# Dividing one more product of a fast matrix multiplication in a hybrid decoder trunk: product 5 in groups 2 to 18

## What is computed

```python
def reference(x, norm_g, w_in, conv_w, conv_b, w_a_out, w_b_out, w_o, final_g):
    h = rmsnorm(x, norm_g[0])                        # x: 1024 positions x 1024 channels
    proj = h @ w_in[0]                               # 1024 x 12288
    b_a, c_a, x_a, z_a, q, k, v, z_b, g_a, g_b = jnp.split(proj, split_points, axis=-1)
    y_a = short_conv_branch(b_a, c_a, x_a, z_a, conv_w[0], conv_b[0], w_a_out[0])
    y_b = retention_branch(q, k, v, z_b, w_b_out[0]) # rotary(q), rotary(k), decay, chunks of 128
    merged = jax.nn.sigmoid(g_a) * y_a + jax.nn.sigmoid(g_b) * y_b
    return rmsnorm(x + merged @ w_o[0], final_g)
```

## Time and profile before

| | |
|---|---|
| median of 3 runs | 1365.6 us |
| the profiled execution's own time | 1365.87 us |
| its span, first to last instruction | 1364.1 us |
| TensorE busy (share of the span) | 1351.8 us (99%) |
| VectorE busy | 1060.0 us (78%) |
| ScalarE, GpSimd busy | 608.3 us, 413.7 us |
| mean DMA rate | 172 GB/s |

### The profile page before, as it was taken

The page is one execution under the profiler, slowest core; times in us unless marked ns, Lnnn a source line. Parts: engine busy times, 40 slices in busy tenths (PEclk is TensorE's granted clock), DMA queues, the critical chain, the costliest instruction groups (busy, mean ns, idle before and its releaser), DMA issues.

```text
span 1364.1 us, 17294 instructions
## 1 busy us (share of the span) xinstructions
PE 1351.8 (99%) x6642; PEld 1142.7 (84%) x6642; DVE 1060.0 (78%) x1097; ACT 608.3 (45%) x821; POOL 413.7 (30%) x381
## 2 busy tenths in 40 slices
PE   9999999999999999999999999999999999999997
PEld 7788888888888888888888888888888888888886
DVE  6898465677878777678888778748776998788887
ACT  6843233433333333333333433438778433433445
POOL 0100112344444554444443444315444001100002
PEclk9999999999999999999999999999999999999999
DMA  9646445344433433476666666757768699945443
GB/s 333 216 132 214 141 110 166 95 108 109 109 101 86 108 93 99 136 183 172 176 162 166 147 166 179 223 201 252 267 223 267 141 332 308 235 158 201 162 85 124
DMA packets 112979, 234.81 MB, mean 172 GB/s; under 512 B 7680, under 2 KB 50816, under 8 KB 108032
## 3 DMA queue, kind: packets, MB, share of 16 engines
q1 hardware_dynamic: 104112, 194.87, 42.2%
q0 software_dynamic: 8640, 38.80, 16.0%
q10 hardware_dynamic: 144, 0.02, 0.0%
HBM read 169.70 MB, written 55.57 MB: 165 GB/s over the span
## 4 chain that ended last, share of the span: by engine, by line
PE 92%; ACT 2%; issue 1%; DVE 1%; DMA 1%; POOL 1%; SPq 1%; POOLq 0%; ACTq 0%; DVEq 0%
PE psum L2625 15%; PE psum L2627 15%; PE psum L2628 15%; PE psum L2768 7%; PE psum L2766 7%; PE psum L2767 7%; PE psum L2549 3%; PE psum L2551 3%; PE psum L2550 3%; PE psum L2538 3%; PE psum L2540 3%; PE psum L2541 3%; PE psum L2670 2%; PE psum L2672 2%; PE psum L2671 2%
## 5 line engine op out<-in xcount | busy, mean ns | idle before, releaser
L1146 ACT ACTIVATE slots<-work 128x1024 fp32r<-128x1024 f32 (+1 forms) x166 | 169.5, 1027 | 418.0 <-PE psum L2628 292.1
L2625 PE MATMUL psum<-hc,slots 128*128 128x512 f32 x912 | 355.0, 389 | 0.0
L2627 PE MATMUL psum<-hc,slots 128*128 128x512 f32 x912 | 354.9, 389 | 0.0
L2628 PE MATMUL psum<-hc,slots 128*128 128x512 f32 x912 | 354.8, 389 | 0.0
L2628 PEld LDWEIGHTS psum<-hc,slots 128*128 128x128 f32 x912 | 171.2, 188 | 35.8
L2625 PEld LDWEIGHTS psum<-hc,slots 128*128 128x128 f32 x912 | 171.2, 188 | 35.3 <-issue 0.4
L2627 PEld LDWEIGHTS psum<-hc,slots 128*128 128x128 f32 x912 | 171.2, 188 | 34.8
L1435 ACT ACTIVATE last_slot<-arena 128x1024 fp32r<-128x1024 f32 x112 | 118.6, 1062 | 163.0 <-PE psum L2768 157.3
L2766 PE MATMUL psum<-last_slot 128*128 128x512 f32 (+1 forms) x452 | 175.3, 388 | 0.0
L2768 PE MATMUL psum<-last_slot 128*128 128x512 f32 (+1 forms) x452 | 175.0, 387 | 0.0
L2767 PE MATMUL psum<-last_slot 128*128 128x512 f32 (+1 forms) x452 | 175.0, 387 | 0.0
(11 more groups left out here) (228 smaller groups left out, 2496.1 us busy)
## 6 DMA issues: line engine op xcount, KB each, us to landing
work<-w_channel SPq DMA_DIRECT2D x80, 512.0 KB, 4.0
work<-w_channel POOLq DMA_DIRECT2D x40, 512.0 KB, 5.5
arena<-w_last SPq DMA_DIRECT2D x19, 1024.0 KB, 7.9
qk<-qk_scratch SPq DMA_DIRECT2D x32, 512.0 KB, 3.4
arena<-w_last POOLq DMA_DIRECT2D x9, 1024.0 KB, 10.5
v_raw<-value_scratch SPq DMA_DIRECT2D x32, 256.0 KB, 3.9
arena<-gate_scratch SPq DMA_DIRECT2D x16, 512.0 KB, 6.8
value_c<-w_value SPq DMA_DIRECT2D x10, 512.0 KB, 4.8
```

Of the source, the lines that this page charges most:

```text
L1146: nc.scalar.activation(slots[:, u % SLOTS, 0, 0:columns_of(u)], src, ACT.Copy, scale=-1.0 if negated(u) else 1.0).then_inc(w_hi, 1)
L2625: nc.tensor.matmul(bank, slot[:, 0, w], x_high, start=product in STARTS and j == 0, stop=False, skip_group_check=True)
L2627: nc.tensor.matmul(bank, slot[:, 0, w], x_low, start=False, stop=False, skip_group_check=True)
L2628: last = nc.tensor.matmul(bank, slot[:, 1, w], x_high, start=False, stop=j == 3, skip_group_check=True)
```

## The change

Product 5 is divided like product 4, in groups 2 to 18 (`FIFTHS`), as two units 5a (place 3) and 5b (`FIFTH_HALF`). x's combinations for the quarters of product 5 are made in group 0 and kept in HBM (`hx_d`, `kept_d`). The buffer `hx` holds those of product 5 and of product 4 in turn: two loads (512 KB for T4, 1024 KB for T1 and T2) twice in each group. T3 stays in the place of a quarter of x, as before. S1 of groups 1 to 19 is no longer added by GpSimd but made in buffer e by a load of quadrant 3 and an adding transfer of quadrant 2. Rotation steps are at other places. The PSUM bank for 5's inner sums is the other group's set.

```diff
-UNIT_TABLE = [(g, p) for g in range(GROUPS) for p in (0, 1, 2, 3, 4, 5, 6, LAST_HALF, THIRD_HALF)
+FIFTHS = range(2, GROUPS - 1)
+UNIT_TABLE = [(g, p) for g in range(GROUPS) for p in (0, 1, 2, 3, FIFTH_HALF, 4, 5, 6, LAST_HALF, THIRD_HALF)
...
-    ROLES.append(dict(a=r["c"], b=r["b"], c=r["a"], d=r["e"], e=r["d"]))
+    ROLES.append(dict(a=r["c"], b=r["b"], c=r["a"], d=r["d"], e=r["e"]))
...
+        def load_hx(product):
+            n = int(product == 5)
+            sp.dma_start(hx[:, 2].bitcast(F32), hx_d[n, :, 2]).then_inc(t4_in, 16)
+            sp.dma_start(hx[:, 0:2].bitcast(F32), hx_d[n, :, 0:2]).then_inc(t1_t2_in, 16)
...
+            if g in FIFTHS:
+                sp.wait_ge(unit_done, ended_at(g - 1) + 1)
+                load_hx(5)
...
-                sp.wait_ge(w_ready, unit_at(g, 5) + 1)
-                load_work(g + 1, "d", 3)
+                sp.wait_ge(w_ready, fifth_ended_at(g) + 1)
+                load_work(g + 1, "e", 3)
...
+                if g in FIFTHS:
+                    sp.wait_ge(unit_done, fifth_ended_at(g) + 1)
+                    load_hx(4)
...
         def s1(g):
+            if g:
+                work_loaded(g, "e")
+                pool.dma_start(work[ROLES[g]["e"]][:, :], w_channel[g, 2], accum_op=ALU.add).then_inc(s1_in, 16)
...
         def s2(g):
+            if g:
+                pool.wait_ge(s1_in, 16 * g)
...
+            if g in FIFTHS:
+                second_sums(g, 5)
             if g in THIRDS:
                 second_sums(g, 3)
...
+                elif n == 3 and halved_product(g, 5):
+                    second_first(g, 5)
+                elif n == FIFTH_HALF:
+                    second_rest(g, 5, range(1))
+                    low(u + 2)
+                    second_rest(g, 5, range(1, 3))
+                    add(g, 5)
...
-                    for step in {0: (0,), 2: (1, 2, 3, 4, 5)}.get(p, ()):
+                    for step in ({0: (0,), 1: (1, 2, 3, 4), 2: (5,)} if g in FIFTHS else {0: (0,), 2: (1, 2, 3, 4, 5)}).get(p, ()):
                         turn(last, 0, step)
                     if p == 3:
                         turned(last, 0)
-                    for step in {3: (0, 1, 2, 3), 4: (4, 5)}.get(p, ()):
+                    for step in ({2: (0, 1), 4: (2, 3, 4, 5)} if g in FIFTHS else {3: (0, 1, 2, 3), 4: (4, 5)}).get(p, ()):
                         turn(last, 1, step)
-                    if p == 4:
+                    if p == (5 if g in FIFTHS else 4):
                         turned(last, 1)
...
+            if product != 3 and g in FIFTHS:
+                pe.wait_ge(t4_in, 16 + 16 * hx_loads(g, product))
             product_of_quarters(u, 2, second(product, "T4"), direct_quarter(g, product, 2)).then_inc(unit_done, 1)
```

More of the change, by code:

```diff
@@ L191 @@
     r = ROLES[-1]
[L192 removed]
+    ROLES.append(dict(a=r["c"], b=r["b"], c=r["a"], d=r["d"], e=r["e"]))
 LOADED = [{n: 0 for n in range(5)}]
 for r in ROLES:
[L195 removed]
+    LOADED.append({n: LOADED[-1][n] + (n != r["e"] or len(LOADED) > 1) for n in range(5)})
 TP_STORES = {"gate": 4, "conv": 0, "turn": 8}
@@ L342, in build @@
     t4_sums = sb("t4_sums", CONS_AT + 8 * KB, [P, 4, 2, QUARTER])
+    t5_high, t5_low = (sb(f"t5_{n}", TP_AT[1] + m * 8 * KB, [P, 4, 2, QUARTER]) for m, n in enumerate(("high", "low")))
     t3_quarters = sb("t3_quarters", CONS_AT, [P, 4, 2, QUARTER])
@@ L716, in _ @@
                 stores[kind_of(g - 1)](g - 1)
+            if g + 1 < GROUPS and g not in THIRDS:
+                sp.wait_ge(w_ready, ended_at(g) + 1)
+                load_work(g + 1, "d", 3)
             if g == QZS.start:
@@ L1547, in _ @@
             g, p = place_of(u)
-            if g == 0 and p == 5:
+            if g == 0 and p == 2:
+                fifth_high()
+            if g == 0 and p == 6:
                 for name in ("T1", "T2", "T4"):
@@ L1836, in second_first, with second_rest @@
             nc.vector.tensor_tensor(at, at, psum[:, second_bank(g, product), 0:QUARTER], ALU.subtract).then_inc(value_sum, 1)
-        def second_rest(g, product):
-            dve.wait_ge(unit_done, (ended_at(g) if product == 4 else third_ended_at(g)) + 1)
+        def second_rest(g, product, parts=range(3)):
+            dve.wait_ge(unit_done, halved_ended_at(g, product) + 1)
             z = second_bank(g, product)
             to = flat((tp_v if product == 4 else tp_first)[g % 2][:, :, :]).rearrange("p (n c) -> p n c", n=4)
-            for n, (quarters, bank, c) in enumerate(((slice(1, 4), z, 0), (slice(1, 4, 2), z + 1, 0),
-                                                     (slice(2, 4), z + 1, QUARTER))):
+            for n in parts:
+                quarters, bank, c = ((slice(1, 4), z, 0), (slice(1, 4, 2), z + 1, 0), (slice(2, 4), z + 1, QUARTER))[n]
                 if n:
@@ L2129, in _ @@
             g, p = place_of(u)
-            if g == 0 and p in (1, 2):
-                for n in range(2):
-                    t4_quarter(2 * (p - 1) + n)
-            if g == 0 and p in (3, 4):
-                for name in (("T1", "T3"), ("T2", "T4"))[p - 3]:
-                    t_sum(name, t4_quarters, t4_sums, 12)
-            if g == 0 and p == 6:
+            if g == 0 and p == 0:
+                for n in range(4):
+                    t5_quarter(n)
+            if g == 0 and p == 1:
+                for name in ("T1", "T3", "T2", "T4"):
+                    t_sum(name, t5_high, t5_low, 12)
+            if g == 0 and p == 3:
+                fifth_low()
+            if g == 0 and p in (2, 4):
+                for n in range(2):
+                    t4_quarter(p - 2 + n)
+            if g == 0 and p == 5:
+                for name in ("T1", "T3", "T2", "T4"):
+                    t_sum(name, t4_quarters, t4_sums, 20)
+            if g == 1 and p == 0:
                 for name in ("T1", "T2", "T4"):
@@ L2592, in unit @@
                 pe.wait_ge(kept_in, 80)
+            if product == 5 and g == FIFTHS.stop:
+                pe.wait_ge(fifth_kept, 192)
             if product == 3 and g == THIRDS.stop:
@@ L2739, in _ @@
                     first_half(g, product)
+                    if product == 5:
+                        second_half(g, 5)
                     if product == 4:
```

144 lines of the change are left out of this document (101 added, 43 removed).

## The result

The changed kernel takes 1387.3 us (median of four runs, 1383.1 to 1388.9) against 1365.8 us before (1365.4 to 1366.3): a ratio of 1.0153, with a 95% interval of 1.0140 to 1.0165. The profiled execution took 1387.9 us, 22 us more than that of before. 1387 lies 7 us over the predicted 1380 and inside its range.

The account below looks back on a forecast made before the run. TensorE's own work bounds the kernel, but VectorE's deadlines decide: -8.7 us of work, 8 x 1.7 rotation stops, 8 x 1.15 convolution stops and 0.6 for group 2 give +14.7, so 1380 us, range 1369 to 1391.

Parts of the forecast that it names:

- The removed work: TensorE, product 5 of 17 groups: a whole product takes 5.44 us, a halved one 4.93, so 8.7 us go in all.
- the 22 us more that the prediction excluded: TensorE: by the skill's weight-load rule halved products would cost 22 us; the measured 117 ns per matmul exclude it.
- The lock: VectorE and GpSimd, both reading two SBUF operands, delay each other by whole instructions; instructions with a PSUM operand are not delayed.
- What VectorE gets: VectorE gets 3.7 us more work per group, in group 13 34.3 of 37.1 us; it fits on average.
- Rotation groups: Groups 11 to 18: second_first comes late for 5b's last quarter product, so TensorE stands 1.7 us in each of 8.
- Convolution groups: Groups 3 to 10: TensorE stands 0.75 us for low(5b) and 0.4 for a late S2, 1.15 us in each of 8.
- I cost it at nothing: Loads of x's combinations: no cost, since loads are issued 17 and 9 to 13 us ahead.
- The share of 0.99: DMA queues in rotation groups: the added loads and addition, a share of 0.36, on 0.63 come to 0.99.
- Rival C: Transfers: share near 1 makes product 4's loads or S1's adding transfer 2 us late in 8 to 16 groups; 1396 to 1412, chance 0.11.
- The five stores and the loads around groups 1 and 2 ... nothing: These transfers cost nothing: more than 10 us before they are needed, against 4 to 8 us to landing.
- The signs that it named: TensorE waits for second_first, some 8 times 1.7 us, and low of 5b, about 8 near 1; second_sums(5) over 4 us.
- TensorE waits for DMA: One of the signs in TensorE's waits that would show the forecast wrong; no size given.

## Why the prediction was right, and where it was off

- **The removed work, right.** 5.44 and 4.93 us held (2.13 + 2.80), 8.7 us in all; the 22 us more that the prediction excluded do not appear. The kernel without sums and loads shows 6.5 us of them in the time; its remaining TensorE waits for changed work come to 1.5 us.
- **The lock, right as a mechanism.** Both engines alternate instruction by instruction, and the order put in by hand met the end of second_first in group 13 to 0.1 us. What VectorE gets was right too: 34.3 us forecast for group 13, 34.74 in the kernel without sums and loads. The Trainium skill (SBUF — State Buffer, "Who interferes with whom") has this lock for a VectorE instruction with two SBUF inputs against a GpSimd one that reads SBUF; the two timelines agree: VectorE's 0.69 us became 1.11 to 1.23 beside GpSimd's additions, while its addition with a PSUM operand, at 671.87, took its usual 1.21.
- **Rotation groups, size off.** The fixed stop is 1.13 us, not 1.7. The working started the alternation of rotation steps 1 to 4 and the additions only once silu had ended (658.85 to 664.0). Without the loads, at the same start of the group (648.8), step 1 is already asked for at 657.54, beside silu, and the last addition ends at 663.36 (the line below): 0.6 us sooner, and second_first is 0.8 sooner. In the changed kernel VectorE's wait of 0.63 us for a landing gives just that back, so that the 0.1 us of agreement in group 13 is partly luck.

GpSimd's last addition of second_sums(5) in group 13 of the kernel without loads:

```profile
662.29 1.07 POOL L1032 TENSOR_TENSOR work<-work 128x256 f32<-128x256 f32 x1
```

- **Convolution groups, size off.** The term was 1.15 us per group. Without the loads it is 0.34. The two parts, 0.75 for low(5b) and 0.4 for S2, were both too large for a calm group: in group 6 of the changed kernel low(5b) starts at 411.43, 17.4 us after the group's start, where the forecast had it start 18.05 after. The 0.4 for S2 is no constant: groups 3, 6, 9 and 10 show nothing of it, and in group 4, whose adding transfer landed after 7.6 us, TensorE stood for 1.6 us at 5b.
- **"I cost it at nothing": the step that failed.** The loads of x's combinations are worth 17.7 us (16.7 counted against the kernel before of the same chip), not 0. The share of 0.99 worked out beside that sentence was measured at 0.90 in group 13, and that was enough. Rival C described it as a case of its own at 1396 to 1412; it is a term of every case. TensorE itself waited for such a load only once, for 1.0 us. The rest went another way: the other loads landed late, and the wait passed to VectorE, to S2 and to group 19.
- **"The five stores and the loads around groups 1 and 2 ... nothing", wrong for group 2.** It took 3.1 us more against 0.1 forecast. A copy of a third combination on ScalarE waited 4 us for a store that had been issued 10.6 us before it could start, low(7) and second_first came after it, and TensorE's clock then fell. Without the loads of x's combinations 0.85 of the 3.1 us remain; without the sums all of them do. The copy, on ScalarE's timeline:

```profile
254.84 0.63 ACT L1322 ACTIVATE third_T<-t_sums 128x512 fp32r<-128x512 f32 x1 [3.97 <-DMA gate_scratch<-tp_v]
```

- **Group 19, not in the sum at all.** Before it issues the first load of q and k, SP waits until earlier stores have landed: 10.0 us here (the line below), 6.2 before. TensorE then stood for 3.7 us until that load had landed. Nothing in the change touches these stores but the queues, which are fuller. Without the loads of x's combinations group 19 has its old length, and with GpSimd's own S1 in place of the adding transfers too; both seem to have a part in it.

SP's longest wait in group 19:

```profile
SPq L828 <- DMA gate_scratch<-tp_v: 10.0, 1, 10.0
```

- **The signs that it named.** second_first stopped TensorE nine times, 1.3 us on average (forecast 8 times 1.7). The low half of 5b did it four times for 1.0 us on average, and by 0.2 in the calm groups (forecast 8 times near 1). second_sums(5) took 4.55 to 4.80 us in groups 3 to 18 (forecast over 4). But "TensorE waits for DMA", which was to show the forecast wrong, came true twice, for 1.0 and 3.7 us.
- **So the 1380 came out of two errors against each other.** The fixed stops were put at 13.6 + 9.2 + 0.6 = 23.4 us and measure 9.0 + 2.7 + 1.4 = 13.1; the landings were put at 0 and measure 17.7. -8.7 + 13.1 = +4.4 against the 4.8 us that the kernel without loads stands over before; with 17.7 it is +22. That the total fell into the range is thus in part luck.

What stays open: how the 17.7 us divide between single landings. They fall on other groups in other runs, and I did not try a version that moves the same bytes at other times.

## What to carry to other kernels

Where the bounding engine is 99% busy, a change that shortens its work has to be costed by the deadlines of the in-order engine that feeds it, with every instruction laid in place under the lock; an average of 34 us in 37 says nothing, and a step moved off one deadline lands on the next. Bytes have to be costed too: here, with a DMA share near 0.9 in the rotation groups, the loads of weights took 5.7 us to land in place of 4.0 (medians of the whole run), and waits that had had a margin became stops, also in group 19, which the change does not touch. A 2 x 2 of kernels, each suspected cost left out alone and both together, tells how much of the cost is in their meeting.

## What was not expected of the hardware

**TensorE's clock fell after short stops.** Three times in the changed kernel's profiled run the granted clock fell to half (1.2 GHz) for 3.4 us, at 262, 720 and 918 us, each time just after TensorE had stood, for 2.07, 1.92 and 3.68 us. Windows around the three:

```profile
260.00:267.00 7.00, 6.01 (x22) 4.93 (x23) 6.68 (x10) 1.36 (x2) 5.04 (x7) 0.76 0.69 253
717.00:724.00 7.00, 5.08 (x19) 4.08 (x19) 6.86 (x10) 2.36 (x4) 2.08 (x3) 0.76 0.65 230
918.00:926.00 8.00, 8.00 (x33) 6.51 (x33) 2.90 (x5) 1.59 (x4) 1.27 (x1) 0.80 0.93 343
```

Product 7 of groups 2 and 14 took 7.08 and 7.07 us against 5.44, so a stop of 2 us costs 3.6. The three come to about 5 us of the 22. Before, the channel groups had none; the kernel without the loads, with its nine stops of 1.1 us, has none either. The traces of the other kernels agree: each of the 19 falls in the channel groups of all traces comes at a stop of 1.83 us or more, no stop of 1.74 us or less is followed by one, and four of 1.93 to 2.40 us are not either. That the stop is the cause is argued from this order of events; no run tried it by itself.

**Spread.** The changed kernel's runs differ by 5.8 us, those of rotation groups alone by 7.7, and those with the gate product moved by 9.1. With the loads out it is 1.0, with sums and loads out 0.4. The kernel before has 0.9 in four runs and 2.2 in fourteen on another chip. The kernels slowed by GpSimd's own S1 or by the later rotation differ by 3.4 and 2.4, with the loads in. Where a kernel waits on late landings, its single runs say little, and an interval from several is needed to tell 5 us.
